# Layer kernel: last expert's one-hot made and turned at the gather, its output in two exact passes, the final norm by halves, and six edits of the front

## What is computed

```python
for layer in range(2):
    proj = rms_norm(h, attn_norm[layer]) @ w_in[layer]
    y = concat(retention_heads(proj), latent_heads(proj))     # 4 and 4 heads of 128
    h = h + y @ w_out[layer]
    hn = rms_norm(h, ffn_norm[layer])
    h = h + (swiglu(hn) if layer == 0 else moe_swiglu(hn))    # top 2 of 8, softmax gates
out = rms_norm(h, final_norm)[:, 16:]
```

## Time and profile before

| | us |
|---|---|
| median of three runs | 1539.18 (1536.52 to 1541.78) |
| profiled execution, its own time | 1540.51 |
| its span, first to last instruction | 1538.5 |
| PE busy | 1513.2 |
| DVE busy | 1233.3 |
| ACT busy | 1013.4 |
| granted TensorE clock, mean | 0.993 of full |

### The profile page before, as it was taken

The page is one execution under the profiler, slowest core; times in us unless marked ns, Lnnn a source line. Parts: engine busy times, 40 slices in busy tenths (PEclk is TensorE's granted clock), DMA queues, the critical chain, the costliest instruction groups (busy, mean ns, idle before and its releaser), DMA issues.

```text
span 1538.5 us, 21849 instructions
## 1 busy us (share of the span) xinstructions
PE 1513.2 (98%) x8362; PEld 1305.5 (85%) x8362; DVE 1233.3 (80%) x1068; ACT 1013.4 (66%) x946; POOL 38.0 (2%) x42
## 2 busy tenths in 40 slices
PE   9999999999999999999999999999999999999997
PEld 9779999999987888888888888888888888888885
DVE  6746776767884568889898888888888888888887
ACT  7655434334574557777777777777777777777775
POOL 0000000000000012000000000000000000000000
PEclk9999999999999999999999999999999999999998
DMA  9314454444324349999999999989999999999992
GB/s 355 134 46 170 159 181 189 178 170 188 117 110 164 137 154 386 393 366 402 373 349 403 377 349 401 386 344 395 391 350 386 391 371 364 397 378 348 422 377 95
DMA packets 64707, 447.91 MB, mean 291 GB/s; under 512 B 8121, under 2 KB 8153, under 8 KB 12432
## 3 DMA queue, kind: packets, MB, share of 16 engines
q1 hardware_dynamic: 61200, 437.49, 72.7%
q0 software_dynamic: 3456, 9.71, 2.2%
HBM read 442.20 MB, written 7.36 MB: 292 GB/s over the span
## 4 chain that ended last, share of the span: by engine, by line
PE 89%; DVE 6%; ACT 4%; issue 1%; ACTq 0%; DVEq 0%; POOL 0%; POOLq 0%
PE bank L501 86%; PE bank L505 3%; DVE w_lo L1240 1%; DVE w_lo L1559 1%; ACT w_hi L1157 1%; ACT w_hi L939 1%; DVE scratch L1298 0%; ACT scratch L1013 0%; ACT scratch L1141 0%; ACT scratch L1014 0%; DVE scratch L1283 0%; DVE r_row L1267 0%; DVE scratch L1287 0%; DVE parts L1254 0%; DVE scratch L1294 0%
## 5 line engine op out<-in xcount | busy, mean ns | idle before, releaser
L501 PE MATMUL bank<-w_hi,parts 128*128 128x512 f32 x2688 | 834.5, 392 | 3.1 <-DVE parts L1543 1.5
L1559 DVE TENSOR_TENSOR w_lo<-ring,w_hi 128x2048 fp32r<-128x2048 f32 x288 | 659.4, 2292 | 93.5 <-ACT w_hi L1157 90.1
L1157 ACT ACTIVATE w_hi<-ring 128x2048 fp32r<-128x2048 f32 x288 | 551.9, 1919 | 173.4 <-PE bank L501 146.0
L501 PEld LDWEIGHTS bank<-w_hi,parts 128*128 128x128 f32 x2688 | 499.7, 188 | 107.7 <-DVE w_lo L1559 4.9
L501 PE MATMUL bank<-w_lo,parts 128*128 128x512 f32 x1344 | 523.8, 390 | 0.0
L501 PE MATMUL bank<-parts,w_hi 128*128 128x272 f32 (+1 forms) x2240 | 432.5, 291 | 3.2 <-DVE parts L1254 1.8
L501 PEld LDWEIGHTS bank<-parts,w_hi 128*128 128x128 f32 x2240 | 354.5, 189 | 4.7 <-DVE w_lo L1240 2.0
L501 PE MATMUL bank<-parts,w_lo 128*128 128x272 f32 (+1 forms) x1120 | 323.0, 288 | 0.0
L501 PEld LDWEIGHTS bank<-w_lo,parts 128*128 128x128 f32 x1344 | 252.2, 188 | 53.3
L501 PEld LDWEIGHTS bank<-parts,w_lo 128*128 128x128 f32 x1120 | 212.4, 190 | 0.4
L1240 DVE TENSOR_TENSOR w_lo<-ring,w_hi 128x2048 fp32r<-128x2048 f32 x71 | 161.3, 2288 | 53.6 <-ACT w_hi L939 53.6
(11 more groups left out here) (180 smaller groups left out, 636.3 us busy)
## 6 DMA issues: line engine op xcount, KB each, us to landing
ring<-stream SPq DMA_DIRECT2D x359, 1024.0 KB, 5.5
...
ring<-stream SPq DMA_DIRECT2D x2, 768.0 KB, 10.1
...
```

The source lines that it names most:

```text
L501: return release(nc.tensor.matmul(dst, lhsT, rhs, start=start, stop=stop), inc)
L1157: A(w_hi[:, n % HSLOTS, :], moe_slot(m), ACT.Copy).then_inc(split_hi, 1)
L1559: V.tensor_tensor(w_lo[:, n % HSLOTS, :], moe_slot(m), w_hi[:, n % HSLOTS, :].bitcast(F32), ALU.subtract).then_inc(split_lo, 1)
```

## The change

The tail: the one-hots of the last expert are made on DVE and turned by PE while the routing is under way (`turn_last`), and DVE copies them before `take(0)`. ACT writes the gated last output as a high part directly, DVE its low part, and PE multiplies each with the one-hots, whose entries are 0 or 1, so that two passes are exact. The outputs come half by half of the width rather than tile by tile. The sum of squares is taken in halves; the first half's sum, with the constant added by DVE, is the bias of the root. The last quarter of the output is multiplied with the gain on DVE and scaled on ACT, and stored by itself.

The front, six edits: (1) half of unit 0 comes ahead of the rows, which come in quarters, and 24 warming products stand in place of 48; (2) `high(b + 8)` comes behind the value copies, `low(b + 8)` behind the second mask; (3) T1 is unit 11, the second gate unit 12; (4) the probabilities of head 0 are turned ahead of the retention values; (5) `low(b + 15)` comes behind the last rows, and `row_scale(1)` ahead of the first low part of the dense layer; (6) `spread` multiplies the 32 rows that hold its head alone, and the four bM stand together, with yR3 behind them.

```diff
@@ -77,7 +77,7 @@
 SLOT_COLS = PASSES + 1
-U_UQ, U_UKV, U_RV, U_RG, U_T1, U_T2, U_WO = 6, 7, 8, 10, 12, 13, 14
+U_UQ, U_UKV, U_RV, U_RG, U_T1, U_RG2, U_T2, U_WO = 6, 7, 8, 10, 11, 12, 13, 14
@@ -96,8 +96,8 @@
  "qn0", "qn1", "qpe0", "qn2", "qpe1", "qn3", "kn0", "kn1", "kn2", "kn3", "v0", "v1", "v2",
- "rT0", "rT1", "rT2", "rT3", "rv0", "rv1", "rv2", "g0", "yM0", "g1", "yM1", "g2", "yM2", "yM3", "yR0", "sM", "yR1", "yR2", "bM0", "bM1",
- "yR3", "bM2", "bM3", "g3", "sR", "bR0", "bR1", "bR2", "bR3"])
+ "rT0", "rT1", "rT2", "rT3", "rv0", "rv1", "rv2", "g0", "yM0", "g1", "yM1", "g2", "yM2", "yM3", "yR0", "sM", "yR1", "yR2", "bM0", "bM1", "bM2", "bM3",
+ "yR3", "g3", "sR", "bR0", "bR1", "bR2", "bR3"])
@@ -169,6 +169,8 @@
 x_lo = parts[:, DK * CAP:2 * DK * CAP].rearrange("p (k c) -> p k c", k=DK)
+y_hi, y_lo = [parts[:, a * D:(a + 1) * D] for a in (4, 5)]
+into_tokens = parts[:, 6 * D:6 * D + FRAMES]
@@ -361,10 +365,19 @@
     sp.dma_start(g_sb[:, :], gains).then_inc(gains_in, 16)
-    for half in range(2):
-        c = slice(half * UNIT // 2, (half + 1) * UNIT // 2)
-        sp.dma_start(hT[:, 4 * half:4 * half + 4, :], h0[:, 4 * half:4 * half + 4, :]).then_inc(x_in[half], 16)
-        sp.dma_start(ring[:, 0, c], stream[0, :, c]).then_inc(slot_in[0] if half else first_in, 16)
+    def load_rows(q):
+        sp.dma_start(hT[:, 2 * q:2 * q + 2, :], h0[:, 2 * q:2 * q + 2, :]).then_inc(x_in[q], 16)
+
+    def load_half(j):
+        c = slice(j * UNIT // 2, (j + 1) * UNIT // 2)
+        sp.dma_start(ring[:, 0, c], stream[0, :, c]).then_inc(slot_in[0] if j else first_in, 16)
+
+    load_half(0)
+    load_rows(0)
+    load_rows(1)
+    load_half(1)
+    load_rows(2)
+    load_rows(3)
@@ -400,10 +413,13 @@
         sp.dma_start(moe_slot(m), stream[MOE_AT + m, :, :]).then_inc(slot_in[m % MOE_SLOTS], 16)
-    for j in range(2):
-        sp.wait_ge(res_ready, j + 1)
-        sp.dma_start(out[j * P:(j + 1) * P, :], res[:, j, :]).then_inc(out_stored, 16)
-    sp.wait_ge(out_stored, 32)
+    sp.wait_ge(res_ready, 1)
+    sp.dma_start(out[0:P, :], res[:, 0, :]).then_inc(out_stored, 16)
+    sp.wait_ge(res_ready, 2)
+    sp.dma_start(out[P:2 * P, 0:512], res[:, 1, 0:512]).then_inc(out_stored, 16)
+    sp.wait_ge(last_half, 1)
+    sp.dma_start(out[P:2 * P, 512:D], res[:, 1, 512:D]).then_inc(out_stored, 16)
+    sp.wait_ge(out_stored, 48)
@@ -651,7 +667,8 @@
             pe.wait_ge(pack_ready, 2 * layer + odd + 1)
-            mm(dst, col(C_ROW + h * P), sq3[:, 2 * odd, :], True, True, out_done)
+            q = slice(32 * h, 32 * h + 32)
+            mm(dst, col(C_ROW + h * P)[q, :], sq3[q, 2 * odd, :], True, True, out_done)
@@ -681,6 +698,7 @@
                 latent_scores(1 + h)
+        prob_transposes(0)
@@ -688,14 +706,13 @@
                 turn(dst[0:rows, h * P:(h + 1) * P], std[:, h, p0:p0 + rows], out_done if h == HEADS - 1 else None)
-        prob_transposes(0)
...
         weigh("yM1", 1, vm)
-        proj("g2", U_RG + 1, 0)
+        proj("g2", U_RG2, 0)
@@ -709,10 +726,10 @@
         spread("bM1")
-        weigh("yR3", 7, rv)
...
         spread("bM3")
-        proj("g3", U_RG + 1, 1)
+        weigh("yR3", 7, rv)
+        proj("g3", U_RG2, 1)
@@ -844,17 +861,24 @@
-    def scatter_last(its):
-
-        pe.wait_ge(xg_ready, its + 1)
+    def turn_last():
...
         for t in range(2):
-            turn(bank[7][:, t * P:(t + 1) * P], G[:, t, :], gwt_done if t else None)
+            turn(bank[3][:, t * P:(t + 1) * P], G_last[:, t, :], gwt_done if t else None)
         pe.wait_ge(gwt_ready, 1)
-        pe.wait_ge(ye_ready, its + 1)
-        for j in range(4):
-            t, half = j // 2, j % 2
-            mm(bank[j][:, :], GWT[:, t * P:(t + 1) * P], ye[:, half * 512:(half + 1) * 512], True, True, sc_out)
+
+    def scatter_last():
+
+        keep_clock(4, 3)
+        for half in range(2):
+            c = slice(half * 512, (half + 1) * 512)
+            pe.wait_ge(y_hi_ready, half + 1)
+            for t in range(2):
+                mm(bank[2 * half + t][:, :], into_tokens[:, t * P:(t + 1) * P], y_hi[:, c], True, False)
+            pe.wait_ge(y_lo_ready, half + 1)
+            for t in range(2):
+                mm(bank[2 * half + t][:, :], into_tokens[:, t * P:(t + 1) * P], y_lo[:, c], False, True, sc_out)
@@ -912,19 +936,20 @@
     pe.wait_ge(ones_set, 4)
-    keep_clock(48)
+    keep_clock(24)
...
     gather_first()
+    turn_last()
...
             expert(r * EXPERTS + e)
-    scatter_last(rounds * EXPERTS)
+    scatter_last()
@@ -948,8 +973,8 @@
             act.wait_ge(h_added, [0, 0, 8 + DK * (CHUNKS - 1)][n] + k + 1)
-        elif k % 4 == 0:
-            act.wait_ge(x_in[k // 4], 16)
+        elif k % 2 == 0:
+            act.wait_ge(x_in[k // 2], 16)
@@ -1046,8 +1071,8 @@
                 A(std[:, 0:2, :], std[:, 0:2, :], ACT.Sqrt).then_inc(mean_rooted, 1)
-            if name in ("q1", "q3", "k1", "k3"):
-                high(b + 5 + ["q1", "q3", "k1", "k3"].index(name))
+            if name in ("q1", "q3", "k1"):
+                high(b + 5 + ["q1", "q3", "k1"].index(name))
@@ -1057,6 +1082,7 @@
             keep(f"v{t}", vm[0:rows, t, :], rows, 512)
+        high(b + 8)
@@ -1178,10 +1204,11 @@
     act.wait_ge(gains_in, 16)
+    high_half(0)
     for k in range(DK):
+        if k == 4:
+            high_half(1)
         row_high(0, k)
-        if k % 4 == 3:
-            high_half(k // 4)
@@ -1210,13 +1237,28 @@
     its = rounds * EXPERTS
-    scatter_copy(its)
+    act.wait_ge(w_used, its * FFN_UNITS + MOE_SPLIT)
+    for half in range(2):
+        A(y_hi[:, half * 512:(half + 1) * 512], bank[4 + half][:, :], ACT.Copy,
+          scale=slot_gate[:, its, :]).then_inc(y_hi_ready, 1)
...
+
+    def square(n):
+        half, t = n // 2, n % 2
+        c = slice(half * 512, (half + 1) * 512)
+        act.wait_ge(acc_added, n + 1)
+        A(res[:, t, c], acc[:, t, c], ACT.Square, scale=D ** -0.5, accum_out=fin[:, t, half:half + 1]).then_inc(fsq, 1)
+
+    square(0)
+    square(1)
     for t in range(2):
-        act.wait_ge(acc_added, 2 * t + 2)
-        A(res[:, t, :], acc[:, t, :], ACT.Square, accum_out=fin[:, t, 0:1]).then_inc(fsq, 1)
-        act.wait_ge(fsq, t + 1)
-        A(fin[:, t, 1:2], fin[:, t, 0:1], ACT.Sqrt, bias=eps_sb[:, 0:1], scale=1.0 / D).then_inc(fstd, 1)
+        square(2 + t)
+        act.wait_ge(fsq, 3 + t)
+        act.wait_ge(fin_eps, t + 1)
+        A(fin[:, t, 3:4], fin[:, t, 1:2], ACT.Sqrt, bias=fin[:, t, 2:3]).then_inc(fstd, 1)
+    act.wait_ge(graded_ready, 1)
+    act.wait_ge(fin_scale, 2)
+    A(res[:, 1, 512:D], graded, ACT.Copy, scale=fin[:, 1, 3:4]).then_inc(last_half, 1)
@@ -1360,13 +1402,14 @@
         rope(7)
-        low(b + 8)
...
             mask_max(h)
+            if h == 1:
+                low(b + 8)
@@ -1412,7 +1455,6 @@
             if layer == 0 and d == 6:
-                low(b + 15)
@@ -1426,6 +1468,7 @@
             row_low(1, 7)
+            low(b + 15)
@@ -1439,8 +1482,6 @@
             if kind == "g":
-                if c == 0:
-                    row_scale(1)
@@ -1508,6 +1549,11 @@
         link(V.tensor_reduce(cnt[:, 0:1], bank[2][:, 16:24], axis=AX.X, op=ALU.max))
+        link(V.tensor_scalar(cnt[:, 1:2], cnt[:, 0:1], float(CAP), -float(CAP), ALU.is_gt, ALU.mult))
+        link(V.tensor_scalar(nxt, route[:, EXPERTS - 1, :], cnt[:, 1:2], None, ALU.add))
+        for t in range(2):
+            x = V.tensor_scalar(G_last[:, t, :], col(C_IOTA, CAP), nxt[:, t:t + 1], None, ALU.is_equal)
+        x.then_inc(g_ready, 1)
@@ -1518,6 +1564,8 @@
         V.memset(bank[5][:, :], 0.0).then_inc(y_zero, 1)
+        dve.wait_ge(gwt_done, 1)
+        V.tensor_copy(into_tokens, bank[3][:, 0:FRAMES]).then_inc(gwt_ready, 1)
@@ -1580,14 +1628,16 @@
     dve.wait_ge(gains_in, 16)
+    low_half(0)
     for k in range(DK):
+        if k == 4:
+            low_half(1)
         row_low(0, k)
-        if k % 4 == 3:
-            low_half(k // 4)
...
     attention(0)
+    row_scale(1)
@@ -1602,20 +1652,28 @@
         dve.wait_ge(round_shifted, r + 1)
-    link(V.tensor_scalar(nxt, route[:, EXPERTS - 1, :], float(CAP), None, ALU.add))
-    for t in range(2):
-        x = V.tensor_scalar(G[:, t, :], col(C_IOTA, CAP), nxt[:, t:t + 1], None, ALU.is_equal)
-    x.then_inc(g_ready, 1)
-    dve.wait_ge(gwt_done, 1)
-    V.tensor_copy(GWT, bank[7][:, 0:FRAMES]).then_inc(gwt_ready, 1)
+    its = rounds * EXPERTS
+    for half in range(2):
+        c = slice(half * 512, (half + 1) * 512)
+        dve.wait_ge(y_hi_ready, half + 1)
+        V.scalar_tensor_tensor(out=y_lo[:, c], in0=bank[4 + half][:, :], scalar=slot_gate[:, its, :],
+                               in1=y_hi[:, c].bitcast(F32), op0=ALU.mult, op1=ALU.subtract).then_inc(y_lo_ready, 1)
     dve.wait_ge(acc_in, 16)
-    for j in range(4):
-        add_out(j)
     dve.wait_ge(fn_in, 16)
+    add_out(0)
+    add_out(1)
+    dve.wait_ge(fsq, 2)
+    V.tensor_scalar(fin[:, :, 2:3], fin[:, :, 0:1], EPS, None, ALU.add).then_inc(fin_eps, 2)
```

(12 more changed lines are left out.)

12 lines of the change are left out of this document (7 added, 5 removed).

## The result

| | before | after |
|---|---|---|
| median of the runs | 1539.18 us (5 runs, 1536.52 to 1542.16) | 1528.73 us (5 runs, 1527.91 to 1531.83) |
| profiled execution: time, span | 1540.51, 1538.5 | 1531.83, 1530.0 |
| PE busy | 1513.2 | 1503.1 |
| PE's granted clock, mean | 0.993 | 0.994 |

The ratio is 0.9935, 95% interval 0.9918 to 0.9952: 10.4 us faster where 8.0 were forecast. A second set of runs of the changed kernel, on a chip where the kernel before took 1540.49, gave 0.9933 (0.9917 to 0.9948). The forecast of 1531.2 is 2.5 high. The rival with overlapping spreads said 1528.5. One run further down, of the kernel with warming products, fell in a slower state of the chip (1603.3 at a granted clock of 0.879) and is left out of its median.

The account below looks back on a forecast made before the run. TensorE, busy 98% of the span, was taken as the bound. Terms -0.8 - 0.4 - 1.2 - 3.4 + 0.8 + 0.9 - 3.9 = -8.0 took 1539.2 to 1531.2 us; range 1526.5 to 1536.0.

Parts of the forecast that it names:

- rival with overlapping spreads: Spreads on different 32-row groups overlap on PE: -2.7, four spreads in 1.2 us, sum -10.7, 1528.5 us; chance 35%.
- start of layer 0: Fewer warming products and reordered loads end ACT's root's wait for PE: -0.8, between 0 and 2.6.
- unit b+8, two layers: Moving ACT's 1.91 us copy from ahead of the query copies gains 0.2 per layer, since DVE's rotations limit: -0.4.
- decay table earlier: T1 loaded a unit earlier: DVE waits for it but PE does not, so nothing gained.
- probability transposes: Six short products fill a PE wait of 0.6 ahead of the value transposes in each layer: -1.2.
- entry of the dense layer: Reordered DVE work removes PE waits of 1.8 and 1.3 and a clock fall, adds a 1.5 wait: -3.4.
- spreads, width and order: Spreading reciprocals over 32 rows on PE costs mode switches of about 0.2 each, without overlap: +0.8.
- routing: Turning and copying the last one-hot delays the low parts before the experts: +0.9, between 0.4 and 1.3.
- tail: From ACT's first tail copy to the last scaling 10.1 us instead of 14.1; third transfer +0.1: -3.9.
- first to last expert product: The experts' stretch, 950 us, with nothing inside its loop touched by the change: no change.
- three signs of being wrong: Experts' stretch changes by more than a microsecond, PE waits at the spreads, or unit 2 lands at another time.
- slow rival: Clock halves at six thin stretches (dense entry's sum, before experts, four spread groups), 1.7 us each: 1541.4 us; chance 3%.

Follow-up runs that it names:

- kernel with warming products: Changed kernel with ACT's gathered-row copies ahead of the Exp, DVE's low parts ahead of its one-hot copy, five warming products before the experts; 1529.80 us.
- the tail alone: The kernel before with only the tail's part of the change, all six front edits undone; 1538.30 us, ratio 0.9989.
- values first: Changed kernel with the first probability transposes behind the value transposes again, as before; 1532.81 us.
- changed, again: The changed kernel itself, unaltered, run and traced a second time; 1529.02 us.
- take and copy: Changed kernel with ACT's copies of the gathered rows ahead of the Exp and DVE's low parts ahead of its one-hot copy; 1529.91 us.

## Why the prediction was right, step by step

| step | forecast | measured by stretches |
|---|---|---|
| start of layer 0 | -0.8 | -0.7 (K 60.88 to 60.2; -0.9 by the means) |
| unit b+8, two layers | -0.4 | -0.3 (0.13 in layer 1, taken twice) |
| decay table earlier | 0 | not tried alone |
| probability transposes | -1.2 | -1.5 |
| entry of the dense layer | -3.4 | -3.5 |
| spreads, width and order | +0.8 | -3.1 |
| routing | +0.9 | +0.9 |
| tail | -3.9 | -3.7 |
| first to last expert product | 0, a fall in the range | +1.3 (some 0.9 of it a fall of the clock) |

The spreads' number is that of both edits together: Y to K' and Y' to R in the kernel before and in the one with the tail alone, against the changed one's undisturbed ones, less the dense entry's 3.5 and unit b+8's 0.1 (366.5 - 361.2 - 3.6 and 64.2 - 62.6). The column sums to -10.6; the two sets of runs gave -10.4 and -11.5. The direction, the range (1526.5 to 1536.0) and six of the terms stand. That the forecast is off by only 2.5 is in part luck: the spreads missed by 3.9, and the 1.3 more in the experts took back a third of it. Of the three signs of being wrong that the prediction named, two came: the experts' stretch moved by more than a microsecond, and unit 2 lands at another time. PE doesn't wait at the spreads.

**The step that failed** is "Spreading the reciprocals over 32 rows". It said "what costs is the switch" and took +0.8. The runs show -3.1. I took the single step between two shapes as the price of each switch, and argued against overlap that each record of a new shape starts only when the one before is through. That row has products on the same rows; nothing in it speaks of products on different ones. Both bounds of the term, -2.7 and +3.2, were in the text, and I took the wrong one as likelier, 42 to 35. The rival named the mechanism right. Its sum of -10.7 keeps the +0.8 for switches beside the -2.7, so its term is -1.9, small by 1.2; that its 1528.5 lies on the measured 1528.7 is luck, since the 1.3 in the experts is not in it. By its own sign, 1.2 us for four spreads, the first group has it (1.26) and the second is well below (0.68): there all four run together, their first records start at 129.50, 129.51, 129.52 and 129.52.

The Trainium skill, TensorEngine Tiling (Array Packing), Key Properties, states both the drain at a change of mode and that different tiles can run in parallel. Here starts 0.01 us apart (117.39, 117.40, 117.41) show the second, and two pairs instead of four in a row cost 0.2 more in both layers together, so that the first is small. The measurement agrees with the page; I weighed its two sentences wrongly.

**Right in size, wrong in reason: the routing.** The +0.9 was put to turning and copying the last one-hot. Those are hidden. The delay comes through the four operations that I called harmless, since they stand ahead of the gates, and ACT's Exp, its table load and its copies hang on these.

**Right: the dense entry**, wait for wait, the clock too. **Right: the tail**, where the third transfer cost 0.4 to 0.5 behind the last scaling instead of 0.1. PE's last products are hidden as said, at full clock: they end at 1520.95, and DVE takes up the second pair of additions only at 1522.16, behind ACT's sums of squares. Whether they would be hidden at half clock no run shows, since in every trace of the new tail the clock falls 3.8 us or more behind the start of the last six records, when they have ended.

**The slow rival** (a fall at each thin stretch) had the right kind of thing and the wrong number: one of its six places, the experts' start, had the fall regularly, and the one behind the sum of squares never. Behind the latent spreads four falls begin, each 1.8 us behind the first spread: at 121.3 and 517.3 (values first), 512.8 (changed, again) and 514.3 (take and copy). That is 4 of the 20 passes with four spreads over 32 rows in a row, and none of the 8 with 128 rows or in pairs; that the edit brings them is neither shown nor ruled out, and where one comes it takes back 1.6 of the 3.1. The query up-projections, which the rival didn't name, had a fall in 8 of 22 passes.
